# Filler products between values and turns in the attentions of head pairs

## The reference, cut to what matters

```
logits = einsum('bnqkgd,bnskd->bnkgqs', qb, kk) * scale - sl * dist     # 128 queries, up to 256 keys
p      = softmax(concat([where(valid, logits, -inf), sink]))[..., :-1]
out    = einsum('bnkgqs,bnskd->bnqkgd', p, vv)
```

## Time and profile before

| what | value |
|---|---|
| device time, median of 3 runs | 1576.77 us (1573.62 to 1582.04) |
| the profiled execution | 1580.49 us |
| its span | 1578.7 us |
| PE busy | 1539.0 us, 97% of the span, 7966 matmuls |
| DVE, ACT, POOL busy | 884.0, 696.2, 261.7 us |
| mean granted TensorE clock | 0.991 of full |
| `sliding` on TensorE | about 555 to 657 us of the span |
| `other_attentions` on TensorE | about 900 to 1055 us |

### The profile page before, as it was taken

One profiled execution on the slowest core, in us unless ns is written; L12 is line 12 of the kernel. 1 busy time (PEld: TensorE's weight loads), 2 busy tenths in 40 slices (PEclk: granted clock), 3 DMA queues, 4 the chain that ended last, 5 costly groups with the idle time before them and its releaser, 6 DMA issues. The chain is left out here.

```text
span 1578.7 us, 21184 instructions
## 1 busy us (share of the span) xinstructions
PE 1539.0 (97%) x7966; PEld 1275.8 (81%) x7966; DVE 884.0 (56%) x1698; ACT 696.2 (44%) x1425; POOL 261.7 (17%) x155
## 2 busy tenths in 40 slices
PE   9999999999999999999999999899989999999998
PEld 8888878887788889888888777778867888888887
DVE  4522299858735666545844577747576444444223
ACT  4322456666423477644335545543264333332123
POOL 0000044165300012200012233213210000000002
PEclk9999999999999999999999999899999999999999
DMA  6226265211322521123431211213212223222321
GB/s 225 97 86 181 93 168 147 87 55 54 107 94 93 147 74 41 44 91 107 137 107 54 67 64 58 94 39 105 97 54 67 94 93 102 98 94 94 104 97 67
DMA packets 49860, 149.19 MB, mean 94 GB/s; under 512 B 6560, under 2 KB 8992, under 8 KB 49632
## 3 DMA queue, kind: packets, MB, share of 16 engines
q1 hardware_dynamic: 43840, 136.34, 26.8%
q10 hardware_dynamic: 5920, 11.51, 2.4%
HBM read 126.98 MB, written 2.10 MB: 82 GB/s over the span
## 5 line engine op out<-in xcount | busy, mean ns | idle before, releaser
L235 ACT ACTIVATE cut_hi<-raw 128x1024 fp32r<-128x1024 f32 x224 | 237.2, 1059 | 516.1 <-PE ps L252 507.4
L241 DVE TENSOR_TENSOR cut_lo<-raw,cut_hi 128x1024 fp32r<-128x1024 f32 x168 | 209.7, 1248 | 427.6 <-ACT cut_hi L235 427.4
L252 PE MATMUL ps<-h_hi,cut_hi 128*128 128x512 f32 (+1 forms) x904 | 359.4, 398 | 5.0 <-DVE cut_lo L241 3.1
L254 PE MATMUL ps<-h_hi,cut_lo 128*128 128x512 f32 (+1 forms) x904 | 351.5, 389 | 0.0
L253 PE MATMUL ps<-h_lo,cut_hi 128*128 128x512 f32 (+1 forms) x904 | 351.1, 388 | 0.0
L241 POOL TENSOR_TENSOR cut_lo<-raw,cut_hi 128x1024 fp32r<-128x1024 f32 x56 | 135.5, 2419 | 455.1 <-ACT cut_hi L235 455.1
L252 PEld LDWEIGHTS ps<-h_hi,cut_hi 128*128 128x128 f32 x904 | 170.2, 188 | 49.1 <-issue 13.0
L254 PEld LDWEIGHTS ps<-h_hi,cut_lo 128*128 128x128 f32 x904 | 170.0, 188 | 36.2
L253 PEld LDWEIGHTS ps<-h_lo,cut_hi 128*128 128x128 f32 x904 | 170.4, 189 | 31.4
L1171 PEld LDWEIGHTS ps<-arena,scr 128*128 128x128 f32 x464 | 64.9, 197 | 11.7 <-issue 5.1
L252 PE MATMUL ps<-ff_hi,cut_hi 128*128 128x512 f32 (+1 forms) x192 | 71.4, 372 | 0.0
(11 more groups left out here) (455 smaller groups left out, 2955.6 us busy)
## 6 DMA issues: line engine op xcount, KB each, us to landing
raw<-weights SPq DMA_DIRECT2D x228, 512.0 KB, 3.2
tiles_r<-tiles_r SPq DMA_DIRECT2D x96, 128.0 KB, 2.3
scr<-scr ACTq DMA_DIRECT2D x34, 64.0 KB, 3.5
xf<-x_in SPq DMA_DIRECT2D x8, 256.0 KB, 7.0
xf<-x_in ACTq DMA_DIRECT2D x1, 2048.0 KB, 8.3
q_stack<-qT_lo ACTq DMA_DIRECT2D x16, 128.0 KB, 2.4
out<-xf SPq DMA_DIRECT2D x8, 256.0 KB, 2.2
consts<-tables ACTq DMA_DIRECT2D x1, 1732.0 KB, 9.3
```

Of the source, the lines that this page charges most:

```text
L235: act.activation(cut_to(u)[0], raw[:, u % RAW, :], ACT.Copy).then_inc(hi_ready, 1)
L241: eng.tensor_tensor(lo, raw[:, u % RAW, :], hi.bitcast(F32), ALU.subtract).then_inc(lo_ready, 1)
L252: a = pe.matmul(out, left[0], right[0], start=start, stop=False, **skip)
L254: return a, pe.matmul(out, left[1], right[0], start=False, stop=stop, **skip)
```

## The change

`pe_turns` splits the filler turns of a step in three pieces in the joint form and in four in the other, and one piece goes between values and turns. The same turns are made in the same order and in the same steps; only TensorE's queue changes.

```diff
-            def pe_turns(step, half):
-                k = first_turn(step + 1) - first_turn(step) if fill else 0
-                return (k + 1) // 2 if half == 0 else k // 2
+            def pe_turns(step, piece):
+
+                k, pieces = first_turn(step + 1) - first_turn(step) if fill else 0, 3 if joint else 4
+                return (k * (piece + 1) + pieces - 1) // pieces - (k * piece + pieces - 1) // pieces
...
                         for g, heads_g in enumerate(groups):
-                            for _ in range(pe_turns(step, g)):
+                            for _ in range(pe_turns(step, 2 * g)):
                                 next(filler, None)
                             if step >= LAG:
                                 i, u = step - LAG, units[step - LAG]
...
                                 last.then_inc(valued, 1)
+                            for _ in range(pe_turns(step, 2 * g + 1)):
+                                next(filler, None)
                             if 2 <= step < n + 2:
...
                                 last.then_inc(turned, 1)
                         if joint:
-                            for _ in range(pe_turns(step, 1)):
+                            for _ in range(pe_turns(step, 2)):
                                 next(filler, None)
```

## The result

The changed kernel takes 1583.03 us in the median of 20 runs (1581.19 to 1588.35), the kernel before 1577.62 us (1573.62 to 1586.71, 20 runs). The ratio is 1.0031 with a 95% interval of 1.0019 to 1.0043: slower by 4.9 us, 3.0 to 6.8, and within the 0.5% that the prediction called no measurable change. The 20 runs of each tell it from zero all the same.

The account below looks back on a forecast made before the run. TensorE, busy in 97% of the span, was taken to bound the kernel. Terms of 0.65 (`sliding`), 0.6, 0.9 (`other_attentions`) and 1.7 (clock) summed to 3.9 us, so 1576.77 + 3.9 = 1580.7 us; range 1571 to 1589.

Parts of the forecast that it names:

- The steady joint steps, 29 moves at no wait: `sliding`, steady part: T one product later in 29 of 32 steps, copy still 0.38 us ahead of V; cost 0.
- Step 21's cut: `sliding`: ScalarE's cut waits for a product behind T; with the product ahead, V's wait goes, -0.2 us.
- The tail, +0.85 and +0.16 on the path: `sliding`, steps 32 to 34, no S as cover: V +0.16 us, the last V +0.85 us, nothing hides it.
- No T moves, so its waits stay: `other_attentions`: no T moves against S or another T, so T's waits for copies stay at 2.6 us.
- Step 13, +0.6: `other_attentions`: V0, one product earlier, waits for VectorE's late output; T0 and all after 0.62 us later, taken as +0.6.
- `second`, +0.9: `other_attentions`, step 18: V0 stands ahead of `second`, VectorE's chain ends 0.89 us later, step 19's wait grows; +0.9 us.
- The clock, +1.7: After step 19's wait, grown to 2.8 us, one more 3.4 us stretch at half clock; +1.7 us, bounds 0 and 6.9.
- Rival 2: The piece between V and T covers T's wait: the 2.6 us go, nothing is lost; 1574 us, chance 0.08.
- Rival 1: Joint form: late copies make V wait 0.3 us in each of 29 steps, 8.7 us; 1589 us, chance 0.12.
- Rival 3: Half-clock stretches of 13.7 us and one of 3.4 do not come, 8.6 us back; 1570.4 us, chance 0.12.
- Rival 4: After the longer wait 13.7 us at half clock in place of 3.4: +5.2 us more, 1586 us, chance 0.10.
- Rival 5: The change does nothing: V0 and the tail find their inputs anyway; 1576.8 us, chance 0.10.

## Why the prediction came out as it did

It said 1580.7 us, 3.9 us slower and not measurable by the 0.5% bound; measured are 4.9 us by the ratio (3.0 to 6.8). The size is in part luck: two errors offset each other. At full clock the traces give 1.84 us for `sliding` and 3.8 for `other_attentions` (1.91 + 0.96 + 0.9), 5.6 us in all, where the waits of the prediction's sum came to 2.2. The 1.7 us for the clock, which no run confirms, stood in for about half of what was missing.

- *The steady joint steps, 29 moves at no wait*: right, no V waits there for a copy. But "the 29 moves cost 0" is wrong: `sliding` is 0.8 us longer besides its tail. That is after a gain of 0.27 us at step 22, so the 29 moves cost some 1.1 us, 0.04 each. This is the term that the sum lacked. I priced a moved product by its own 0.69 us and by waits, and took the seams to be the same in any order. They are not: V, T, product, S, product became V, product, T, S, product, and S costs 0.08 us more behind T than behind a product (0.56 us to the next product, and not 0.48), of which V gives back some 0.03, since a product starts sooner behind it than T (0.81 and 0.84 us); 3.15 us a step became 3.19.
- *Step 21's cut*: right. The copy there no longer holds up V, and the step of that V takes 2.98 us in place of 3.25: 0.27 us gained, 0.2 forecast.
- *The tail, +0.85 and +0.16 on the path*: right, 1.02 us when taken back, and the barrier did pass it on.
- *"No T moves, so its waits stay"*: right, 2.6 and 2.1 us. The seams again were missing: 1.9 us, 0.5 of them at step 14 alone.
- *Step 13, +0.6*: the wait of V0 was right, 0.28 us of it read as TensorE idle. The term was too small, 1.0 to 1.1 us, since the moved turn is also the last gate product, for whose reading by ScalarE the next turn waits. A moved instruction was followed to those who wait for V and T, and not to those who wait for the instruction itself.
- *`second`, +0.9*: right, 2.79 for 1.89 us.
- *The clock, +1.7*: not confirmed. The clock's share rose by 1.3 us with a standard error of 1.0. In the profile 3.4 us came at 1017, where I had put them, and by all profiles such a stretch follows a wait of 2.8 us more often than one of 1.2. But it cost 0.8 us there and not 1.7: at full clock T of step 19 waits 0.56 us for a copy (in the changed kernel with the small matmuls earlier), a wait that is gone in this profile. The 13.7 us at 993 went away, for which the sum had nothing.

Rival 2, that the piece covers the wait of T, is excluded by the waits of T. Rival 1, late copies, by the absence of V's waits in the middle. Rival 3 had its mechanism in the profile (the stretches at 658.7 and at 993 both go), but not its gain. Rival 4 is not borne out: no profile has 13.7 us at half clock at the wait of step 19; the longest there are 6.8 us, in three of the five with a wait of 2.8. Its chance was also counted wrongly: its own time, 1586, lies 9 us over the kernel before and so beyond the 7.9 us bound, and all of it, not a third, belongs to "slower by over 0.5%". Rival 5, no effect, is excluded by the interval and by the waits of V.

What stays open is what decides the clock from one kernel and run to the next. A wait of 1.2 us at step 19 in place of 2.8 went with a clock's share of 7.6 us in one kernel, and of 11.8 to 12.2 us in the three others with the same wait. Shares of 7.6 to 16.1 us among kernels that differ in the order of a few turns are further apart than the cost of any mechanism measured here.

## What to carry to other kernels

Moving filler between two dependent groups helps only if it changes the distance to whoever makes the input: write down, for each wait, what lies between the releaser and the waiter in a whole cycle, before and after. Then follow the moved instruction itself: who waits for its result, and what covered that. Where the engine is hardly ever idle the order can have a price of its own at the seams between kinds of work, as here, so read the start-to-start times over a full cycle of both orders, and compare stages only between executions that had the same clock there.

## What was not expected of the hardware

- The same 22 matmuls of a step took 3.15 us in one order and 3.19 in another without any wait. In the other form, a product of 128x512 moved from ahead of a group of 128x64 values to behind it cost 0.05 us each time (56.43 to 57.33 us over 18 groups). A turn of twelve small matmuls moved in the same way cost 0.27 us (5.26 to 5.80 us over two groups, in one step).
- The 13.7 us at half clock from 993.20 cost `other_attentions` about 5.5 us: it took 154.62 us with them, and 148.49 in the kernel with the small matmuls earlier, 0.67 us of which are a shorter wait. The 3.4 us at half clock from 1017 cost 0.8 us and not 1.7, where at full clock TensorE waits 0.56 us in the same work.
- Half clock at 993 stood in three of the four profiles in which the first group's products were where they had been, and in none of the nine in which they were moved in steps 14 and 15. Other stretches stood in some profiles and not in others, some ahead of every edit (345.80), over 600 us from it. With one profiled execution of each kernel, no run shows that the edits brought those.
